# Bringing y into the PSUM sum by an identity matmul, and letting ACT copy it out, for eight output tiles

## What is computed

```python
h = rms_norm(x, pre_norm_g[0])
qa, ka, va, qb, kb, vb, ga, gb = split(h @ w_in_ab)
y = concat([diff_attention(qa, ka, va) * silu(ga),       # A: units A0 to A3
            sliding_window_gqa(qb, kb, vb) * silu(gb)])  # B: units B0 to B7
y = y @ w_out_ab                                         # sum over the units, 128 rows of w_out each
x = x + rms_norm(y, post_norm_g[0])
h = rms_norm(x, pre_norm_g[1])                           # layer 1, kind C, in the same way
```

## Time and profile before

| | |
|---|---|
| median of 3 runs | 1225.23 us (1224.18 to 1225.33) |
| profiled execution, its own time | 1223.95 us |
| span in its profile | 1222.2 us |
| PE busy | 1182.2 us, 97% of the span |
| DVE busy | 804.6 us, 66% |
| ACT busy | 588.9 us, 48% |
| granted TensorE clock, mean | 0.995 |

### The profile page before, as it was taken

How to read it: one execution, slowest core, us unless ns; L and a number is a source line. 1 busy time by engine, 2 the same in 40 slices (tenths; PEclk the granted TensorE clock), 3 DMA queues, 4 the chain that set the end, 5 groups by cost and what they waited for, 6 DMA issues and landing times.

```text
span 1222.2 us, 17651 instructions
## 1 busy us (share of the span) xinstructions
PE 1182.2 (97%) x6492; PEld 1006.7 (82%) x6492; DVE 804.6 (66%) x1708; ACT 588.9 (48%) x1296; POOL 432.8 (35%) x557
## 2 busy tenths in 40 slices
PE   7999999999999999898999999999999999999995
PEld 6988888888888887787788888888888888888873
DVE  5464765757767768867553866848658577585585
ACT  5554444434444556655454444534434444454463
POOL 5333214133172465556752114124141241412312
PEclk9999999999999999999999999999999999999998
DMA  6261101011021153245221102011020110201026
GB/s 197 67 192 44 60 18 52 18 53 35 18 87 53 51 156 104 69 127 155 61 77 58 34 21 71 18 56 53 18 74 19 56 53 19 73 18 57 18 47 109
DMA packets 93559, 78.42 MB, mean 64 GB/s; under 512 B 3073, under 2 KB 83969, under 8 KB 93474
## 3 DMA queue, kind: packets, MB, share of 16 engines
q1 hardware_dynamic: 92466, 73.63, 19.9%
q0 software_dynamic: 1008, 3.67, 1.9%
HBM read 68.85 MB, written 13.68 MB: 68 GB/s over the span
## 4 chain that ended last, share of the span: by engine, by line
PE 48%; DVE 2%; issue 1%; ACT 1%; POOL 1%; POOLq 0%; DVEq 0%; ACTq 0%
PE dense L1126 25%; PE dense L1137 7%; PE pv_ps L1259 6%; PE scores L1339 4%; PE turned L1306 4%; PE turned L1294 0%; DVE pT_lo L1836 0%; ACT k_hh L1440 0%; DVE e_sb L1771 0%; POOL w_lo L978 0%; POOL rowstat L1004 0%; DVE fin L2032 0%; PE scores L1137 0%; ACT junk L1622 0%; POOL rowstat L1001 0%
## 5 line engine op out<-in xcount | busy, mean ns | idle before, releaser
L1126 PE MATMUL dense<-hT_hi,w_hi 128*128 128x512 f32 x880 | 350.5, 398 | 0.0
L1126 PE MATMUL dense<-hT_lo,w_hi 128*128 128x512 f32 x880 | 344.6, 392 | 0.0
L1126 PE MATMUL dense<-hT_hi,w_lo 128*128 128x512 f32 x880 | 344.2, 391 | 0.0
L971 POOL TENSOR_SCALAR w_hi<-w_f 128x1024 fp32r<-128x1024 f32 x86 | 93.0, 1081 | 642.4 <-PE dense L1126 585.2
L978 POOL TENSOR_TENSOR w_lo<-w_f,w_hi 128x256 fp32r<-128x256 f32 x344 | 264.8, 801 | 7.2
L1447 ACT ACTIVATE e_sb<-e_sb,low 128x256 f32<-128x256 f32 (+7 forms) x256 | 170.3, 665 | 172.5 <-DVE low L1771 170.1
L1480 ACT ACTIVATE pT_hi<-turned 128x640 fp32r<-128x640 f32 (+3 forms) x224 | 117.2, 523 | 165.3 <-PE pv_ps L1259 94.5
L1126 PEld LDWEIGHTS dense<-hT_hi,w_lo 128*128 128x128 f32 x880 | 165.4, 188 | 36.6
L1126 PEld LDWEIGHTS dense<-hT_hi,w_hi 128*128 128x128 f32 x880 | 166.0, 189 | 26.1 <-issue 0.3
L1126 PEld LDWEIGHTS dense<-hT_lo,w_hi 128*128 128x128 f32 x880 | 166.2, 189 | 25.1
L1836 DVE TENSOR_TENSOR pT_lo<-turned,pT_hi 128x640 fp32r<-128x640 f32 (+3 forms) x224 | 133.5, 596 | 39.1 <-ACT pT_hi L1480 38.9
(11 more groups left out here) (215 smaller groups left out, 1796.7 us busy)
## 6 DMA issues: line engine op xcount, KB each, us to landing
w_f<-in_w_in_c SPq DMA_DIRECT2D x37, 512.0 KB, 4.1
w_f<-in_w_in_ab SPq DMA_DIRECT2D x34, 512.0 KB, 3.9
rel_tiles_dram<-rel_rows_dram SPq DMA_DIRECT2D x1, 5120.0 KB, 23.8
bias<-rel_tiles_dram SPq DMA_DIRECT2D x8, 640.0 KB, 5.5
y<-in_x SPq DMA_DIRECT2D x8, 512.0 KB, 8.0
hT_lo_f<-in_x SPq DMA_DIRECT2D x8, 512.0 KB, 7.2
out_x<-y SPq DMA_DIRECT2D x8, 512.0 KB, 3.9
w_f<-in_w_out_c SPq DMA_DIRECT2D x8, 512.0 KB, 3.7
```

The source lines that it names most:

```text
L971: ts(hi, src, 1.0, 1.0, ALU.mult, ALU.mult).then_inc(w_hi_done, 1)
L1126: last = mm(dense[:, x.n % 2, :], lhs[:, d * P:(d + 1) * P], rhs[:, d, x.f * HALF:(x.f + 1) * HALF], start=i == 0, stop=i == 23)
```

## The change

For the eight output tiles of the pair B[2] and B[3] (`carried(x)`), TensorE opens the sum in bank 2 with one more matmul, `ident` times the tile's part of `y`, and the six matmuls of the tile add to it. Bank 2 then holds the finished rows of `y`, ACT copies it over `y` at the head of its next step and gives the bank back, and DVE has nothing to do for these tiles.

```diff
+def carried(x):
+
+    return x.what == "out" and x.units[-1] is B[3]
...
@@ tensor, spare_use
+                if carried(x):
+                    mm(dense[:, 2, :], ident[:], y[:, x.row, x.half * HALF:(x.half + 1) * HALF], start=True, stop=False)
                 last = out_matmuls(dense[:, 2, :], [(yT_hi, yT_lo, u.col(x.row), hi_place(w.hi)[:, x.half, :], lo_place(w.slot)[:, x.half, :])
-                                                    for u, w in zip(x.units, x.blocks)])
+                                                    for u, w in zip(x.units, x.blocks)], carried(x))
@@ scalar
+        def carried_out(x):
+            if new(s_spare, x.use + 1 - PRO_USES):
+                act.wait_ge(s_spare, x.use + 1 - PRO_USES)
+            copy(y[:, x.row, x.half * HALF:(x.half + 1) * HALF], dense[:, 2, :], ACT.Copy).then_inc(bank_free[2], 1)
+
...
             for x in LATE_AT.get(s - 1, []):
                 if x.what == "turn":
                     hi_of_rows(x)
+                if carried(x):
+                    carried_out(x)
@@ vector
         def spare_use(x):
+            if carried(x):
+                return
```

## The result

| | before | with the change |
|---|---|---|
| median | 1224.69 us (5 runs, 1222.97 to 1225.33) | 1230.95 us (5 runs, 1230.42 to 1231.70) |
| span of the profiled execution | 1222.2 us | 1229.9 us |

The ratio is 1.0051, 95% interval 1.0037 to 1.0065: the change costs 6.3 us, and 4.5 to 8.0 us are within the interval. The forecast was +6.0 us on the earlier median of 1225.23 us, 1231.2 us.

What follows compares the result with a forecast made beforehand. TensorE was taken as the bound in the eight-tile stretch: 6.88 us for eight identity matmuls less 0.87 us of waits gives +6.0 us on the 1225.23 us median, 1231.2 us, range 1229.0 to 1233.4.

Steps and rivals of the forecast that it cites:

- The bound: Stretch making the eight tiles: TensorE busy 34.02 of 34.35 us, so each added matmul is paid unless it fills a wait.
- The price of the identity matmul: Eight plain float32 128x512 matmuls on TensorE: two passes of 0.43 us, 0.86 us each, 6.88 us in all.
- 0.66 and 0.94: Bounds in us for one identity matmul, by recorded starts alone and by summed length; 5.3 and 7.5 us for eight.
- The rival by which it costs like any other 128x512 matmul: Identity matmuls at 0.23 us each, 1.84 us for eight; kernel +0.97 us, 1226.2 us; chance 0.04.
- The two waits: TensorE's lost time around the third (0.35 us) and seventh tile (0.52 us); both were to go, gaining 0.87 us.
- a matmul that waits for the bank cannot fill the wait for the same bank: Eight tiles on TensorE: the identity matmul cannot hide in the 0.87 us of waits, so nothing hides its price.
- stay as they are, since it is behind the wait: Distances from a tile's end to TensorE's next need of the bank: claimed unchanged by the new matmul ahead of every tile.
- The work behind the copy on ACT: Transposed probabilities' copy, pv_ps row and exponential come up to 0.6 us later; cost nothing, or 4.8 us without cover.
- The rival of a late ACT: At the third, fifth and seventh tile ACT's copy comes too late: 1.6 us of TensorE waits, 1232.8 us; chance 0.08.
- What stays behind the stretch: TensorE's 2.60 us wait for hT_lo and the clock fall after it (1.72 us lost) were to be carried along.
- The relief of DVE: Rival: lighter DVE reaches the norm chain behind the stretch, recovering 9.1 us against 6.88; 1223.0 us; chance 0.02.
- The busy time of DVE: Eight adds of about 0.69 us removed from DVE: some 5.5 us less busy.

Runs made afterwards that it cites:

- e1: Changed kernel with the identity matmul kept, but DVE instead of ACT copying the bank into y; 1230.52 us against 1224.75 for the kernel before, ratio 1.0047.
- e2: Changed kernel with ACT's copies but without the identity matmul, so part of y's sum is left out; 1223.67 us against 1224.75 for the kernel before.
- e7: As e6, with DVE also reading row 0's first transposed half ahead of scaling row 1; 1225.63 us against 1224.89 for the kernel before.
- e6: Kernel before, with DVE adding the second tile ahead of q_st and the sixth ahead of the norm-gain multiplication; 1224.99 us against 1224.89, ratio 0.9997.
- e8: As e7, with row 0's second transposed half also read ahead of DVE's multiply-add of row 2; 1226.51 us against 1224.65 for the kernel before.

## Why the prediction was right, and where it was not

*The bound.* Right. TensorE was full in the stretch, and work added to it came out at the end. The tile stretch splits into 7.07 us for the eight matmuls (33.95 - 26.88) less 0.90 us of waits, 6.17 us; the long stretch is 6.01 us longer, the time 6.3 us.

*The price of the identity matmul.* Right in mechanism and size. I took 2 passes of 0.43 us from four instructions at the kernel's end, and rejected 0.66 and 0.94; the doubled matmul measured 6.85 us for eight, 0.86 each, and the first eight 7.07 us, 0.88 each. That it is the type is shown by the float32r matmul at the same place, 0.23 us. The rival by which it costs like any other 128x512 matmul is refuted.

*The two waits.* Right in size, wrong in the reason. I had 0.87 us from the distances of starts; ACT alone gives 0.90, DVE's adds moved forward 0.90. The step that failed reads "a matmul that waits for the bank cannot fill the wait for the same bank". That is true of the bank's next tile and beside the point: a longer tile moves the end of the tile before away from DVE's q_st, and e1, with no copy on ACT, shows the same 33.95 us. So the part of the change that was to pay for part of the matmul, the copy on ACT, pays for nothing in the eight tiles; that the forecast counted 0.87 us for it and the sum still came out is luck. I had the distances "stay as they are, since it is behind the wait"; they do, from one tile's end to the next tile's start, but what DVE still has to do before the add is fixed by the end of the projection, and from there to the tile's end it now has 0.86 us more.

The prediction gave a cause only for the wait at the third tile. At the seventh it was DVE's multiplication by the norm's gain, and it was long that time. The timeline of DVE in the kernel before, there and at the next row:

```profile
470.55 1.69 DVE L1984 TENSOR_TENSOR y<-y,g_post 128x1024 f32<-128x1024 f32 x1
472.16 0.68 DVE L1735 TENSOR_TENSOR y<-dense,y 128x512 f32<-128x512 f32 x1
...
479.86 1.22 DVE L1984 TENSOR_TENSOR y<-y,g_post 128x1024 f32<-128x1024 f32 x1
```

The add ended at 472.84, and TensorE wanted the bank at 472.47, one matmul after 472.24. With 1.22 us for the multiplication the add would have ended at about 472.37, by my estimate just in time. So the larger of the two waits hung on one long instruction. The last section has more on it.

*The work behind the copy on ACT.* Right: neither the changed kernel nor e2 shows a wait of TensorE in the stretch. The rival of a late ACT is refuted; its tightest place, the eighth tile, had ACT's copy start at 482.14 and last 0.60 us, and the tile after it began at 484.51.

*What stays behind the stretch.* Right in the main for this change: the wait (2.60, then 2.48 us) and the fall of the clock behind it moved along. The three windows from 495 to 501 us in the changed kernel:

```profile
495.00:497.00 2.00, 0.73 (x4) 0.73 (x5) 1.97 (x6) 0.35 (x1) 1.92 (x2) 0.82 0.04 11
497.00:499.00 2.00, 2.00 (x11) 2.00 (x10) 1.97 (x4) 1.46 (x5) 2.00 (x4) 0.50 0.00 0
499.00:501.00 2.00, 2.00 (x11) 1.66 (x11) 2.00 (x5) 0.88 (x4) 1.45 (x1) 0.83 0.18 63
```

Granted 0.82, 0.50 and 0.83, which is (0.18 + 0.50 + 0.17) x 2 / 0.5 = 3.4 us at half speed, as before it. The prediction put what ACT's copies do behind the stretch at nothing; it was 0.15 us (64.83 us in e1, 64.68 with them). This nearly cancels the 0.2 us by which the eight matmuls cost more than forecast. That the long stretch gives 6.01 us and the forecast's sum the same is the luck of these two. The relief of DVE did not reach the norm chain: DVE idled instead at the head of the steps, 13.0 us in all, waiting for scores:

```profile
DVE e_sb L1787 <- PE scores L1346: 13.0, 8, 2.7
```

But the reason I gave, that DVE had worked off its adds and the chain is started by a projection's end, is half of it. The run e7 shows that from there on DVE's own work is the bound for about 8 us.

*The busy time of DVE.* I expected 5.5 us less; it was 4.1 us in the stretch and 2.0 us over the span. Each add is recorded with 0.69 us but overlaps its neighbour, which starts about 0.6 us after it (457.12 and 457.73 before), so eight free some 4.9 us at most. The rest over the whole span lies outside the stretch: DVE is busy 1.25 us more ahead of it, where both programs are the same, and 1.0 us more behind the long stretch. What made it so I did not trace, and no run was made for it.

*The number for time.* Forecast 1231.2, measured 1230.95. The difference between the medians, 6.3 us, agrees with the 6.0 us of the sum within the interval. The profiled spans alone differ by 7.7 us and would have misled: the start alone differs by 2.3 us.

## What to carry to other kernels

Where TensorE has no idle time, as in this stretch, an identity matmul that brings an accumulator into PSUM is paid in full, and in plain float32 it cost nearly four times a float32r matmul of the same shape (0.86 and 0.23 us); it stood against waits of 0.35 and 0.52 us at two of eight places. Where an engine gives a bank back too late, look first at what stands ahead of the release in its own program: moving two adds ahead of the job that stood before them removed both waits with no work added, though a third of the gain was lost again behind the stretch. And before a wait is credited to one half of a change, run each half alone; here each half alone removed the same two waits, and only one of them cost TensorE anything.

A version that clearly beats the kernel before was not found. The one with both adds ahead (e6) is 0.56 us shorter in its long stretch, and equal to it by time.

## What was not expected of the hardware

The granted clock in the first 20 us differs between executions of one program. In the changed kernel's first profile the matmuls 128x256 at 17.24 to 18.30 us start 0.21 us apart and last 0.41 us, where those of the kernel before start 0.12 apart and last 0.28, yet the granted clock in the record is 1.00 for both. The windows of the second profiles show the low clock there (0.67 and 0.50 before, 0.63 and 0.52 with the change). Behind the stretch, too, the starts lie twice as far apart where the clock is granted at 0.50: 128x512 matmuls in e8 at 500.39, 500.82 and 501.25, for 0.23 us at 1.00. So the record of the clock seems to have missed a low stretch here, and the distance of starts is the surer sign:

```profile
17.24 0.41 PE L1103 MATMUL dense<-hT_hi,w_hi 128*128 128x256 f32 x1
17.45 0.41 PE L1103 MATMUL dense<-hT_lo,w_hi 128*128 128x256 f32 x1
```

The distance over the eight tiles, on the other hand, repeated to 0.01 us between executions of one program, so that effects of 0.1 us can be read in a trace where the time as a whole scatters by 2 us (1222.97 to 1225.33).

A DVE instruction's length was not constant. The scaling of a row (128x1024 `float32`, inputs and output in SBUF) took 1.27 us at 484.40 in the changed kernel and 1.44 us at 494.06, 1.56 us in the kernel before, and 1.75 and 2.15 us in e6 and e7. The windows view of the changed kernel over the first two (the columns as above, POOL the last of the busy times):

```profile
484.40:485.60 1.20, 1.20 (x6) 0.63 (x4) 1.20 (x2) 1.01 (x2) 0.10 (x1) 1.00 0.02 7
494.00:495.50 1.50, 0.00 (x0) 0.00 (x0) 1.46 (x2) 0.00 (x0) 1.50 (x2) 1.00 0.74 222
```

POOL was idle but for 0.10 us during the short one, and splitting weights (w_hi, w_lo) without a gap during the longer one, as it was in the windows of the other three (2.02 of 2.10 us in e7). The Trainium skill, page "SBUF — State Buffer", section "Who interferes with whom", says that a DVE instruction with two SBUF inputs contends with a GpSimd instruction that reads SBUF. These rows agree with it as far as they go. DMA, which the two windows also differ in (0.02 and 0.74), doesn't go with the length: in the window of the longest, in e7, its share is 0.13.

The long multiplication of the kernel before (1.69 us from 470.55) fits too, and its rows show both sides. The timeline of POOL there:

```profile
468.31 2.85 POOL L978 TENSOR_TENSOR w_lo<-w_f,w_hi 128x256 fp32r<-128x256 f32 x4
471.24 1.05 POOL L1001 TENSOR_SCALAR rowstat<-rowstat 128x1 f32<-128x1 f32 x1
...
475.76 0.19 POOL L1001 TENSOR_SCALAR rowstat<-rowstat 128x1 f32<-128x1 f32 x1 [2.84 <-ACT junk L1622]
```

DVE's instruction began while POOL was splitting, up to 471.16, and took 0.47 us more than at 479.86. POOL's next one has a single element a partition and takes 0.19 us at 475.76, but took 1.05 here and ended at 472.29, with DVE's at 472.24. In the changed kernel the same small instruction took 0.78 us from 477.36 and ended at 478.14, with DVE's multiplication at 478.10. That POOL is the cause was not tested by a run, and how much one POOL instruction costs, 0.17 or 0.88 us, these rows do not settle.
